# Small buffers placed behind the large ones in a two-block network on one core

## The reference

```python
# first block: layer 0 is latent attention, layer 1 gated linear attention
hx = rms_norm(x, norm_g[i]) * (1 + scx) + sx          # scx, sx, gx from c @ ada_w
yc, yx = mla_mixer(hc, hx, ...)                       # i = 0: softmax attention, 16 heads
yc, yx = gla_mixer(hc, hx, ...)                       # i = 1: chunked scan, 4 heads
x = x + gx * yx
# second block: two layers, each a mixer and a convolutional FFN of width 2816
y = rmsnorm(h, mix_norm_g[layer])
mix = jnp.concatenate([a_out, b_out], -1) @ ev_w_out[e]        # layer 0: S5 and gMLP
mix = shortconv_mixer(y @ od_w_in[o], ...) @ od_w_out[o]       # layer 1
h = h + mix
h = h + conv_ffn(rmsnorm(h, ffn_norm_g[layer]), ffn_w_up[layer], ...)
return rmsnorm(h, final_norm_g)
```

## Time and profile before

| | us |
|---|---|
| median of 3 runs | 2364.95 |
| the runs | 2364.10, 2364.95, 2368.47 |
| the profiled execution | 2368.89 |
| its span, first to last instruction | 2367.10 |
| PE busy | 2066.5 |
| DVE busy | 1143.4 |
| ACT busy | 819.1 |
| POOL busy | 689.7 |

### The profile page before, as it was taken

How to read it: one execution, slowest core, us unless ns; L and a number is a source line. 1 busy time by engine, 2 the same in 40 slices (tenths; PEclk the granted TensorE clock), 3 DMA queues, 4 the chain that set the end, 5 groups by cost and what they waited for, 6 DMA issues and landing times.

```text
span 2367.1 us, 27756 instructions
## 1 busy us (share of the span) xinstructions
PE 2066.5 (87%) x10852; PEld 1683.4 (71%) x10852; DVE 1143.4 (48%) x1717; ACT 819.1 (35%) x1113; POOL 689.7 (29%) x304
## 2 busy tenths in 40 slices
PE   4899999999969789778484879999979997999997
PEld 3787878778858677667273658788758875878875
DVE  3331666666457577576699243313332524331332
ACT  3253232332233444543331243324332324332332
POOL 1121000000312232232135424444333542444442
PEclk9799999999979799889697989999989998999998
DMA  7111111111111101112120213332222321322321
GB/s 277 36 54 45 63 54 63 55 63 63 63 47 39 33 28 45 36 29 92 34 69 18 80 63 98 89 98 90 89 80 81 99 89 57 103 85 92 99 82 52
DMA packets 46545, 167.72 MB, mean 71 GB/s; under 512 B 5424, under 2 KB 5552, under 8 KB 46160
## 3 DMA queue, kind: packets, MB, share of 16 engines
q1 hardware_dynamic: 44496, 159.93, 21.1%
q10 hardware_dynamic: 1920, 6.02, 0.7%
HBM read 163.83 MB, written 2.10 MB: 70 GB/s over the span
## 4 chain that ended last, share of the span: by engine, by line
PE 72%; DVE 20%; ACT 5%; issue 2%; DMA 1%; ACTq 0%; POOL 0%; DVEq 0%
PE ps L430 19%; PE ps L431 19%; PE ps L432 19%; PE ps L527 4%; PE ps L537 3%; DVE ex L1116 2%; PE ps L558 2%; DVE hf L1116 2%; DVE acc L1116 2%; DVE sq L1116 2%; DVE Alo L1116 1%; DVE hf L1122 1%; ACT sq L792 1%; DVE tmp L1116 1%; PE ps L464 1%
## 5 line engine op out<-in xcount | busy, mean ns | idle before, releaser
L1100 POOL TENSOR_TENSOR wlo<-raw,whi 128x1024 fp32r<-128x1024 f32 x253 | 616.5, 2449 | 1550.2 <-ACT whi L775 1550.2
L430 PE MATMUL ps<-Ahi,whi 128*128 128x512 f32 (+1 forms) x1328 | 529.8, 399 | 43.9 <-issue 23.5
L431 PE MATMUL ps<-Alo,whi 128*128 128x512 f32 (+1 forms) x1328 | 522.8, 394 | 0.0
L432 PE MATMUL ps<-Ahi,wlo 128*128 128x512 f32 (+1 forms) x1328 | 517.0, 389 | 0.0
L775 ACT ACTIVATE whi<-raw 128x1024 fp32r<-128x1024 f32 x253 | 259.9, 1055 | 701.2 <-PE ps L432 680.2
L430 PEld LDWEIGHTS ps<-Ahi,whi 128*128 128x128 f32 x1328 | 257.6, 194 | 121.8 <-issue 38.9
L432 PEld LDWEIGHTS ps<-Ahi,wlo 128*128 128x128 f32 x1328 | 257.3, 194 | 54.1
L431 PEld LDWEIGHTS ps<-Alo,whi 128*128 128x128 f32 x1328 | 258.3, 194 | 47.8 <-issue 0.2
L1122 DVE SCALAR_TENSOR_TENSOR cv<-ps,vec,cv 128x511 f32<-128x511 f32 (+1 forms) x176 | 131.9, 750 | 320.6 <-ACT cv L792 315.9
L430 PE MATMUL ps<-Fhi,whi 128*128 128x512 f32 x416 | 167.3, 402 | 12.9 <-DVE Flo L1116 12.8
L431 PE MATMUL ps<-Flo,whi 128*128 128x512 f32 x416 | 165.5, 398 | 0.0
(11 more groups left out here) (231 smaller groups left out, 3227.3 us busy)
## 6 DMA issues: line engine op xcount, KB each, us to landing
raw<-in_units SPq DMA_DIRECT2D x301, 512.0 KB, 3.6
X<-in_xT ACTq DMA_DIRECT2D x1, 2048.0 KB, 12.8
out_xT<-X SPq DMA_DIRECT2D x8, 256.0 KB, 2.0
CX<-in_ctxT ACTq DMA_DIRECT2D x1, 1024.0 KB, 15.1
masks<-in_masks ACTq DMA_DIRECT2D x1, 512.0 KB, 3.5
gmw<-in_gmw ACTq DMA_DIRECT2D x1, 384.0 KB, 2.8
bs<-in_bs ACTq DMA_DIRECT2D x1, 384.0 KB, 3.8
vec<-in_vec ACTq DMA_DIRECT2D x1, 312.5 KB, 4.5
```

What stands on the lines that cost most here:

```text
L430: nc.tensor.matmul(out, sh, mh, start=first, stop=False)
L431: nc.tensor.matmul(out, sh, ml, start=False, stop=False)
L432: return nc.tensor.matmul(out, sl, mh, start=False, stop=last)
L1100: nc.gpsimd.tensor_tensor(wlo[:, s % CONV, :], raw[:, plan.unit_at[("split", s)] % RAW, :], whi[:, s % CONV, :].bitcast(fp32), ALU.subtrac ...
```

## The change

The order of the `sb` buffers is another. vec, small2, eps1 and sel go behind the others, mod and sc1 ahead of them, and a buffer that nothing uses, rest, is added at the end. Its size makes the words of vec (NV = 625), of small2 and eps1 (4) and of sel (2) up to a multiple of 32 words; it comes to 9 words, 36 bytes. As the placed buffers lie behind all of these, they move too. Nothing else is touched: the same instructions are issued by the same engines in the same order, on buffers of the same shapes.

```diff
@@ -317,16 +317,16 @@
         raw = sb("raw", [RAW, UT * P])
         whi, wlo = sb("whi", [CONV, UT * P], fp22), sb("wlo", [CONV, UT * P], fp22)
         X = sb("X", [KD, T])
-        vec = sb("vec", [NV])
         ident, ones = sb("ident", [P]), sb("ones", [2 * P])
         hf = sb("hf", [2, N])
         sq = sb("sq", [3, N])
         acc, rstd = sb("acc", [N]), sb("rstd", [N])
-        small2 = sb("small2", [2])
-        eps1 = sb("eps1", [2])
-        mod = sb("mod", [2, 48])
-        sc1 = sb("sc1", [2, 16])
+        mod, sc1 = sb("mod", [2, 48]), sb("sc1", [2, 16])
+        vec = sb("vec", [NV])
+        small2, eps1 = sb("small2", [2]), sb("eps1", [2])
         sel = sb("sel", [2])
+        rest = -(NV + 4 + 2) % 32
+        sb("rest", [rest])
 
         CX = place(0, "CX", [KD, TC])
         rope = place(2048, "rope", [T])
```

## The result

The changed kernel takes 2388.45 us (median of 6 runs, 2383.22 to 2394.71) where the kernel before, run beside it, takes 2365.87 (6 runs, 2364.10 to 2368.47). The ratio is 1.0097, with a 95% interval of 1.0086 to 1.0109: 22.6 us slower. I had forecast 2365, 2358 to 2374. The sign is that of rival A, which I had priced at 17 us.

The account below looks back on a forecast made before the run. The prediction took TensorE's matmul spacing to bound the kernel and priced all three address moves at nothing: 2364.95 + 0 + 0 + 0, so 2365 us, range 2358 to 2374.

Parts of the forecast that it names:

- rival A: 512-column products on Ahi and Fhi turn to the long spacing with rows at 64: +17 us, 2382; chance 0.17.
- What bounds the kernel: TensorE's matmul spacing: 72% of the chain; a 512-column product takes 686.7 or 700.0 ns.
- The layout: Addresses worked out: raw stays at byte 192; placed buffers go from 87808 to 87872, from 0 to 64 past a multiple of 128.
- rival D: Layout differs, raw on a multiple of 128, large operands going from 64 to 0: worth nothing; within the 0.70 for no effect.
- Step 1: Large moving operands of the matmuls go from 0 to 64 past a multiple of 128: price 0.
- Rival C: Each stretch's spacing is drawn anew: 3 to 5 us a run, some 2 a median; within the 0.70 for no effect.
- Rival B: Alternating 512- and 256-column pairs (stages on Hhi and Chi) turn short: 8 us faster, 2357; chance 0.13.
- The signs: Trace tests set beforehand: 512-column products on Ahi and Fhi at only 686.7 or 700.0 ns; a third spacing refutes step 1.
- Steps 2 and 3: Small buffers going from 32 to 64, and the engines' other operands and DMAs, above all CX's load: price 0 each.

Follow-up runs that it names:

- e1: The kernel before with 64 unused bytes behind its last small buffer, so only the placed (large) buffers move, to 64 past a multiple of 128; 2387.67 us, 1.0094.
- e3: The changed kernel with 64 unused bytes ahead of raw, so everything, whi and wlo too, starts on multiples of 128; 2386.77 us, 1.0095.
- e4: The kernel before with 64 unused bytes ahead of raw: whi and wlo on multiples of 128, placed buffers at 64; 2366.70 us, 1.0010.
- e2: The changed kernel with 64 unused bytes behind its last buffer, rest: placed buffers back on multiples of 128, small ones at 64; 2390.16 us, 1.0113.
- g2: The kernel before with only the activations of the FFNs and short convolution at distance 0 (Fhi, Flo moved 192 bytes; new Bhi, Blo); 2357.60 us, 0.9970.
- f2: The kernel before with 192 unused bytes behind its small buffers, distance 0 mod 256 from weights to activations; 2360.33 us, 0.9979.
- h1: The changed kernel with 128 unused bytes behind rest, so its placed buffers are at distance 0 mod 256 from the weights; 2360.44 us, 0.9977.
- g1: The kernel before with Fhi and Flo alone moved by 64 bytes (cv behind them by 256), distance 128 for products on Fhi; 2369.51 us, 1.0019.
- g3: The kernel before with wlo ahead of whi and 64 unused bytes between: distance 128 to wlo, 64 to whi; 2386.31 us, 1.0095.

## Why the prediction was wrong

**What bounds the kernel** was right: PE's matmuls, by their spacing, and two prices of 686.7 and 700.0 ns in the kernel before.

**The layout** was right: the tables of addresses in the two programs have raw at byte 192 in both and the placed buffers from 87808 and 87872 on. The large operands went from 0 to 64 past a multiple of 128, and rival D is out. But I drew from it only that nothing would be gained.

**Step 1 is the step that failed.** It priced the move of the large moving operands at 0, and they cost 18.1 us at full clock in the profiled execution (14.5 and 3.6 above); e1, where nothing else moves, costs 22.4 by the medians. I compared operands at 64 with operands at 0 and found equal numbers. In every row of before, though, one operand of the pair was at 64 and the other at 0: weights at 64 against activations at 0 in the products on Ahi, and the same two with exchanged roles in the v and mv tiles. The change put both at 64, and no row of before has that. I treated the place as a property of one buffer, where e3 and e4 show that it is the distance of two. The rows even held the hint: the v tiles' 700.0 was not the long spacing of the others, but what distance 192 costs, and e2, which exchanged the distances, exchanged the numbers.

**Rival A** had the sign, and the bound that step 1 gave it, +13.3 ns on each short product, was nearly the size: 17 us against 22.6. That is luck in part. Its condition, a spacing that settles after pauses at 64, was not the cause: e4 has the large operands at 64 and is fast, e3 has them at 0 and is slow, and 697 to 700 ns is the mean in every stretch of 512 columns at distance 128. Its own products, those of 512 columns at full clock, cost 14.5 and not 17 us; missing from it are the 256-column products (3.6 us) and what stands at half clock or at a pause (7.1 us, whose cause is open). I gave it 0.17 and cut the range off at half of its price, since I took the rows for evidence against it.

**Rival C** has some truth: at distance 64 a whole stretch can take 700.0 in one execution and 686.7 in another, and at 128 it takes 697.1 or 700.0. e4's 63 products on Fhi took

```profile
1519.14:1563.24 44.10, 25.05 (x64) 11.93 (x63) 1.00 0.29 96
```

700.0 ns, where the kernel before had 686.7. With 512 columns I saw next to none of that at distances 0 and 192. What picks the one or the other is open.

**Rival B** fell here (only the v tiles got shorter, by 3.5 ns), but g2 and f2 show that there is room below 686.7, in the dense stretches: 680 ns.

**The signs.** I had written that step 1 is wrong if a third spacing appears, and it did: a mean of 696.5 ns in the v tiles and of 697 in several stretches on Ahi and Fhi, and 356.0 with 256 columns, where the kernel before had 686.7 or 700.0, and 340.0. The count of products in rival A also leaves out 64 of 512 columns on ghi.

**Steps 2 and 3** held. e1, where the small buffers stay, and the changed kernel agree (2387.67 and 2388.45), and so do f2 and h1 (2360.33 and 2360.44). CX is the first link of the chain in the changed kernel as well:

```profile
4.04 15.52 DMA CX<-in_ctxT
```

It lands 0.3 us later than in the earlier trace rows. At 686 us nothing of it is left. Its place is not what costs this: in g1 and g2 CX lies on the same bytes as before, and the load took 15.80 and 15.63 us; in the eleven kernels where it lies elsewhere, 15.27 to 15.73. The Trainium skill's account of 256-byte boundaries (DMA: Bandwidth & Descriptors, How a descriptor splits into AXI transactions) would give 0.1 us for this load, by the estimate in the prediction; that is smaller than this spread, so no run here confirms or refutes it.

## What to carry to other kernels

Where PE's spacing bounds a kernel, look at the address of the weights and of the activations together: shift one against the other by 64 bytes at a time over 256 and measure, before and after any change of layout, since an innocent small buffer between them can cost 1%. Of the distances measured here, 0 was best for moving rows of 512 float32r columns and 192 for 256 columns, where 0 was the worst, and stages can be placed separately. A row of the trace that shows an operand at a new place is evidence only if its partner is at the new place as well.

## What the runs showed of the hardware

- A float32r matmul of 128 x 128 by 512 columns costs, with its weight load, 226.7 ns (680.0 / 3) to 234 ns (702.2 / 3) from start to start at a granted clock of 1.00 (2.4 GHz), depending on the distance of its two operands mod 256 bytes. Steps of 32 bytes matter: 0, 32, 64, 96 gave 680, 700, 687, 700 ns for three.
- The Trainium skill, TensorE: Matmul & The Clock Gate, section Step-by-step: what each phase is for, says that loading the next tile's weights doesn't take SBUF read bandwidth from the running matmul. Here the spacing depends on where the weights lie relative to the moving rows, by some 3% (680.0 to 702.2 ns); with both on the same bytes mod 256 it is smallest for 512 columns and largest for 256. In the stretches on Ahi TensorE alone reads the moving rows; ScalarE and GpSimd fill other slots of whi and wlo meanwhile, but raw, whi and wlo lie on the same bytes in the kernel before, e1 and f2, and the spacing differs. This suggests that the weight load and the matmul's own read meet somewhere on the way from SBUF; that they do, and where, was not shown.
- A stretch of one and the same program can settle at one of two spacings: 686.7 or 700.0 ns at distance 64, 697.1 or 700.0 at 128. What picks it is open.
- The effect of one operand in three being moved is not a third: g3, with wlo alone at 128, took 2386.31 us, as long as with all at 128 (2387.67).
- The VectorE and ScalarE instructions of the earlier trace rows did not depend on the place of their buffers mod 128, at 32, 64 or 0, beyond 1 to 3 ns (692 against 693, 1057 against 1060).
